# The last four units of an output stage run by token halves, and the next stage's whole half 0 is normed and split behind half 1

## The reference, cut to what matters

```
for li in range(2):
    m = mixer(rms_norm(x, g[0]))            # layer 0: gMLP, layer 1: RG-LRU
    x = x + rms_norm(m, g[1])
    f = (silu(h @ w_g) * (h @ w_u)) @ w_out # h = rms_norm(x, g[2])
    x = x + rms_norm(f, g[3])
```

## Time and profile before

| | us |
|---|---|
| median of 3 runs | 1548.31 |
| lowest and highest | 1547.86, 1551.93 |
| the profiled execution, its own time | 1548.71 |
| its span | 1547.2 |
| PE busy in the span | 1504.1 (97%) |
| DVE, ACT, POOL busy | 1072.6, 698.4, 328.0 |
| granted TensorE clock, mean over the span | 0.989 of full speed |

### The profile page before, as it was taken

One profiled execution on the slowest core, in us unless ns is written; L12 is line 12 of the kernel. 1 busy time (PEld: TensorE's weight loads), 2 busy tenths in 40 slices (PEclk: granted clock), 3 DMA queues, 4 the chain that ended last, 5 costly groups with the idle time before them and its releaser, 6 DMA issues.

```text
span 1547.2 us, 28460 instructions
## 1 busy us (share of the span) xinstructions
PE 1504.1 (97%) x10818; PEld 1477.8 (96%) x10818; DVE 1072.6 (69%) x1481; ACT 698.4 (45%) x1099; POOL 328.0 (21%) x282
## 2 busy tenths in 40 slices
PE   7999999999999999999999998999999999999997
PEld 7999999999999898999999998999989999999996
DVE  6454576766344689999963538967579999975434
ACT  5344432224343455555552534484555555554433
POOL 0100033333000332222210004724133222220003
PEclk9999999999999999999999999999999999999998
DMA  7322233232222112232242341312203423233211
GB/s 236 103 78 67 80 108 92 83 97 86 74 91 83 55 55 83 82 108 81 81 136 70 96 110 37 100 42 88 77 14 82 109 81 108 81 96 108 87 39 65
DMA packets 170507, 133.48 MB, mean 86 GB/s; under 512 B 4888, under 2 KB 147504, under 8 KB 170292
## 3 DMA queue, kind: packets, MB, share of 16 engines
q1 hardware_dynamic: 168756, 128.30, 27.8%
q0 software_dynamic: 1664, 3.95, 0.9%
HBM read 128.92 MB, written 3.29 MB: 85 GB/s over the span
## 4 chain that ended last, share of the span: by engine, by line
PE 87%; DVE 8%; issue 2%; ACT 1%; DMA 1%; POOL 0%; SPq 0%; DVEq 0%; ACTq 0%
PE ps L545 62%; PE ps L834 25%; DVE acc L1345 1%; DVE hl L1376 1%; DVE yb L1589 1%; DVE slo L1724 1%; DVE wide L1589 1%; DMA stage<-in_ffn_w_in_dram 1%; DVE acc L1355 1%; DVE wlo L1659 0%; DVE mixc L1642 0%; DMA wide<-in_x_prompt_dram 0%; PE ps L615 0%; DVE mixc L1641 0%; ACT whi L957 0%
## 5 line engine op out<-in xcount | busy, mean ns | idle before, releaser
L545 PE MATMUL ps<-hh,whi 128*128 128x288 f32 x2112 | 552.1, 300 | 13.7 <-DVE hl L1376 6.7
L545 PE MATMUL ps<-hh,wlo 128*128 128x288 f32 x2112 | 543.9, 296 | 0.0
L545 PE MATMUL ps<-hl,whi 128*128 128x288 f32 x2112 | 543.2, 296 | 0.0
L545 PEld LDWEIGHTS ps<-hh,whi 128*128 128x128 f32 x2112 | 372.1, 189 | 21.5 <-DVE hl L1376 10.3
L545 PEld LDWEIGHTS ps<-hl,whi 128*128 128x128 f32 x2112 | 372.2, 190 | 0.6
L545 PEld LDWEIGHTS ps<-hh,wlo 128*128 128x128 f32 x2112 | 372.5, 190 | 0.0
L1328 DVE TENSOR_TENSOR wlo<-stage,whi 128x1024 fp32r<-128x1024 f32 (+2 forms) x168 | 195.3, 1169 | 252.3 <-ACT whi L957 252.0
L957 ACT ACTIVATE whi<-stage 128x1024 fp32r<-128x1024 f32 (+2 forms) x168 | 165.3, 994 | 401.4 <-PE ps L545 382.4
L834 PE MATMUL ps<-shi,whi 128*128 128x288 f32 x576 | 170.5, 296 | 5.8 <-ACT tmp L1195 5.8
L834 PE MATMUL ps<-slo,whi 128*128 128x288 f32 x576 | 170.9, 297 | 0.0
L834 PE MATMUL ps<-shi,wlo 128*128 128x288 f32 x576 | 170.7, 296 | 0.0
(11 more groups left out here) (196 smaller groups left out, 2281.7 us busy)
## 6 DMA issues: line engine op xcount, KB each, us to landing
stage<-in_ffn_w_in_dram SPq DMA_DIRECT2D x88, 512.0 KB, 4.1
stage<-in_ffn_w_out_dram SPq DMA_DIRECT2D x40, 512.0 KB, 4.5
stage<-in_gm_w_in_dram SPq DMA_DIRECT2D x32, 384.0 KB, 3.9
stage<-in_gm_w_in_dram SPq DMA_DIRECT2D x24, 512.0 KB, 3.7
stage<-in_gm_w_out_dram SPq DMA_DIRECT2D x24, 512.0 KB, 3.7
stage<-in_rg_w_in_dram SPq DMA_DIRECT2D x16, 512.0 KB, 4.5
stage<-in_rg_w_out_dram SPq DMA_DIRECT2D x8, 512.0 KB, 3.9
wide<-in_x_prompt_dram SPq DMA_DIRECT2D x2, 1024.0 KB, 7.4
```

The lines of the kernel that those rows point to most:

```text
L545: return pe.matmul(out, w, x, start=start, stop=stop)
```

## The change

In the second group (G = 1) of every output stage the last four units run by token halves, not the last two (in RO, which has four units, the last three). So half 0 is complete four half-units before half 1 (three in RO). The splits of the next stage's tiles 0, 1 and 2 move behind the end of the units whose slots they take: the first, second and third of the four, in half 1. All eight `normed` and all eight `low` of half 0 move ahead of the four `post_add` of half 1 on DVE, and the `high` of half 0 likewise moves on ACT between and ahead of half 1's `y_out`. A new semaphore counts half 0's copies out, and PE's first tiles wait for it, and for half 1's copies only when they come to half 1. No computation is added or removed. In DMA, the loads of tiles 4 to 6, which wait for the low split of tiles 0 to 2, are issued later.

The diff, cut to its core:

```
-                    for j in range(per - 2):
+                    split = max(per - 2 - 2 * G, 1)
+                    for j in range(split):
...
-                        for j in (per - 2, per - 1):
+                        for j in range(split, per):
...
-                                if (G, h, j) == (1, 1, per - 2):
-                                    if m == 1:
-                                        post_sums(p, 0)
-                                    if m == 3:
-                                        post_spread(p, 0)
+                                if (G, h, j, m) == (1, 1, split, 1):
+                                    post_sums(p, 0)
+                                if (G, h, j, m) == (1, 1, split, 3):
+                                    post_spread(p, 0)
...
-                    pe.wait_ge(pair_free[m], free0[name][m])
+                    pe.wait_ge(y_half_out, 8 * p + 4 + m + 1)
...
+                        if k == 0:
+                            pe.wait_ge(pair_free[m], free0[name][m])
                         part(m, 1, k)
...
                                     post_std(p, 0)
                                     if NEXT[name]:
-                                        split_hi(n + 3)
+                                        split_hi(n + 1)
                                     post_rb(p, 0)
                                     if NEXT[name]:
                                         high(NEXT[name], 0, 0)
-                                if (G, h, m) == (1, 1, 1) and NEXT[name]:
-                                    high(NEXT[name], 0, 1)
+                                        split_hi(n + 2)
+                                        high(NEXT[name], 0, 1)
+                                        high(NEXT[name], 0, 2)
+                                        split_hi(n + 3)
+                                        for k in range(3, 6):
+                                            high(NEXT[name], 0, k)
+                                if (G, h) == (1, 1) and m < 2 and NEXT[name]:
+                                    high(NEXT[name], 0, 6 + m)
...
                                     post_diag(p, 0)
+                                    if NEXT[name]:
+                                        split_lo(n + 1)
                                     normed(p, 0, 0, add=x0_ready if NEXT[name] else x_last[0])
                                     if NEXT[name]:
                                         normed(p, 0, 1)
-                                        split_lo(n + 3)
                                         low(NEXT[name], 0, 0)
-                if NEXT[name]:
-                    normed(p, 0, 2)
+                                        split_lo(n + 2)
+                                        for k in range(1, KD):
+                                            if k + 1 < KD:
+                                                normed(p, 0, k + 1)
+                                            low(NEXT[name], 0, k)
+                                            if k == 2:
+                                                split_lo(n + 3)
...
                 for k in range(1, 4):
-                    normed(p, 0, k + 2)
-                    low(name, 0, k)
                     post_add(p, 1, 1, k)
-                normed(p, 0, 6)
-                low(name, 0, 4)
+                split_lo(n + 3)
                 post_diag(p, 1)
-                normed(p, 0, 7)
-                low(name, 0, 5)
-                split_lo(n + 3)
-                low(name, 0, 6)
                 normed(p, 1, 0)
                 normed(p, 1, 1)
-                low(name, 0, 7)
```

More of the change, by code:

```diff
@@ L296, in trunk_kernel @@
         ptok_done, pstd_ready, prtok_ready = sem("post_tok_done"), sem("post_std_ready"), sem("post_rtok_ready")
+        y_half_out = sem("first_half_copied_out")
         pdiag_ready, pbc_done, prb_ready = sem("post_diag_ready"), sem("post_bc_done"), sem("post_rb_ready")
@@ L796, in first_tiles @@
                         pe.wait_ge(lo_ready, n + 4)
-                        pe.wait_ge(pair_free[3], free0[name][3])
+                        pe.wait_ge(y_half_out, 8 * p + 8)
                         for before in range(k):
@@ L1004, in y_out @@
                 y_copy = act.activation(yo(p, r)[:, half(h)], src, ACT.Copy)
-                if h == 1:
-                    y_copy.then_inc(pair_free[m], 1)
+                y_copy.then_inc(pair_free[m] if h else y_half_out, 1)
             def h_high(k, layer, i, at):
@@ L1114, in out_phase @@
                     n = base[name] + s
-                    if n > base["GO"] and n + 2 < base["END"]:
+                    if n > base["GO"] and n + 2 < base["END"] and s + 2 < 2 * per:
                         split_hi(n + 2, width_of(n + 2))
@@ L1152, in first_tiles @@
                 j, p, n = PRE[name], PRE[name] - 1, base[name]
-                high(name, 0, 2)
                 act.wait_ge(unit_done, n)
                 y_out(p, 1, 1, 3)
-                high(name, 0, 3)
                 post_std(p, 1)
-                high(name, 0, 4)
                 split_hi(n + 3)
-                high(name, 0, 5)
                 post_rb(p, 1)
-                high(name, 0, 6)
-                high(name, 0, 7)
                 for k in range(KD):
@@ L1559, in out_phase @@
                     n = base[name] + s
-                    if n + 2 < base["END"]:
+                    if n + 2 < base["END"] and s + 2 < 2 * per:
                         split_lo(n + 2, width_of(n + 2))
```

## The result

The changed kernel takes 1553.38 us in the median of 20 runs, the kernel before 1548.88 in 20 runs beside them: a ratio of 1.0026, with a 95% interval of 1.0019 to 1.0033. That is 4 us slower: a small loss, but its interval lies wholly above 1. The forecast was 1552.3, its range 1545 to 1557.

A forecast was written before the change was run, and what follows sets the result against it. PE was taken as the bound, movable only in its idle time and slow stretches; the three transitions gave -0.1, +2.4 and +2.4 us, their last piece -0.7, together +4.0 on 1548.7; as median 1552.3, range 1545 to 1557.

The forecast's parts named there:

- P: Start of PE's token sums of half 1 in each transition; forecast 1.8, 1.8 and 3.0 us later than before.
- piece 4: From half 1's last `low` to the next `rb`; half of one half-clock loss of 1.5 us goes away, -0.7 us.
- Half 0's lead: First transition: half 0's last square comes 6.24 us earlier, of which 4.4 are left at the first `normed`.
- PE's wait and the clock: Before half 1's sums, PE's scattered waits become one of about 5.5 us, and the clock falls each time.
- P to S: From the start of half 1's token sums to half 1's first `normed`; forecast 6.4 us in each transition.
- its floor of 5.0: Least time from half 1's sums to its first `normed`: sums, split, root, diagonal, spread and `rb`, 5.0 us.
- The rival in which the clock stays: Clock holds behind PE's wait, sums to half 1's first `normed` take 5.0 us: 1548.1 us, chance 0.13.
- Piece 3: From half 1's first `normed` to its last `low`; one `low` of half 0 is gone from it, -0.4 us.
- What was counted as free: Last unit's weights, later DMAs of tiles 4 to 6 and POOL's earlier adds cost nothing; FO1 gains nothing.
- The rival in which the lead is kept: DVE runs its pairs without waiting for ACT and POOL, and the clock stays: 1540.7 us, chance 0.14.

The follow-up runs named there:

- depth2: The changed kernel with PE's order of before: two units by halves in place of four (three in RO); ACT and DVE orders unchanged; 1563.35 us, 1.0087.
- adds_first: The changed kernel with half 1's squares on ACT and adds on DVE ahead of half 0's `high` and `low` 3 to 7; 1543.94 us, 0.9958.
- filler: The changed kernel with 40 more matmuls on PE just ahead of half 1's token sums, in its 5.6 us wait; 1548.52 us, 0.9994.
- sums_later: The changed kernel with PE's token sums of half 1 behind k = 4 instead of 2, the spread behind k = 5 instead of 4; 1550.10 us, 1.0003.
- split_behind: The changed kernel with tile 0's low split on DVE behind the first `normed` and its residual add, in the first two transitions; 1552.78 us, 1.0022.
- before_adds: The kernel before with half 1's squares ahead of `high` 1 to 3, its adds ahead of `low` 1, PE's sums and spread one step earlier; 1550.03 us, 1.0010.
- adds_first_d2: adds_first with PE's order of before: two units by halves in place of four (three in RO); 1564.11 us, 1.0094.
- before_adds_hold: before_adds with the extra matmuls of hold in the last steps of half 1; 1551.15 us, 1.0007.
- hold: adds_first with extra matmuls on PE where it waits for `low` in the last steps of half 1; 1538.13 us, 0.9928.
- hold_sb: hold and split_behind together, with the edits of both; 1538.94 us, 0.9924.

## Why the prediction was right

The direction, the mechanism and the size were right; two terms of the sum were mis-sized. P came 1.6 us later over the three transitions than forecast and piece 4 was 2.3 us shorter; that they nearly cancel is luck.

- **Half 0's lead.** Forecast: last square 507.23, tile 0's split 511.03, first `normed` 513.3, first `low` 514.8. Measured 507.44, 511.24, 513.48 and 515.09, with an entry 0.14 later. From the entry 4.4 of 6.24 us were left, as forecast. depth2 shows that the lead is real, adds_first where it goes.
- **P, mis-sized.** +1.8, +1.8 and +3.0 were forecast, +2.2, +2.2 and +3.7 measured, inside the bounds of +3.0 and 4.2. The last `low` ended 0.2 later in its place, behind four waits of DVE of 0.28 to 0.29 us for ACT's `high`, and the last square waited 0.42 for the first add. 0.1 is a slip in the sum: 528.2 and 2.0 make 530.2, not 530.1. The third transition lost 0.25 more because its first `normed` came 2.9 us earlier than before (14.89 from the entry for 17.79), 1.46 less than in the first transition, where 1.2 had been counted. 0.2 of that is tile 0's split, which needs no unit of half 1 there but still stands between the diagonal and the `normed` on DVE: from half 0's sums to the `normed` it is 3.0 us, for 2.8 before.
- **PE's wait and the clock.** One wait of about 5.5 forecast, 5.6 measured, and the clock fell in all three. P to S was taken at 6.4 and measured at 6.3, 6.1 and 7.1, and its floor of 5.0 was met by filler to 0.04 us. The rival in which the clock stays did not happen; filler shows what it would have given: 0.9994 of the kernel before, or 1 us less, where 1548.1 had been worked out, 0.2 less. The three transitions after differ in when the clock rose again: from 3.3 to 5.3 us behind P it was at 0.61 and 0.72, and at 0.50 in the third.
- **Piece 3.** -0.4 forecast, -0.41 to -0.46 measured.
- **Piece 4, mis-sized.** -0.7 forecast, with -3.0 as the bound; the bound was met. In piece 3 PE is busy for 15.30 of 15.62 us, where it had waited 1.5 of 16.20. PE's waits at the end of half 1, before and after:

```profile
551.31 0.40 PE L545 MATMUL ps<-hh,whi 128*128 128x288 f32 x1 [1.04 <-DVE hl L1376]
...
552.41 0.40 PE L545 MATMUL ps<-hh,whi 128*128 128x288 f32 x1 [0.44 <-DVE hl L1376]
...
552.74 0.40 PE L546 MATMUL ps<-hh,whi 128*128 128x288 f32 x1 [0.44 <-DVE hl L1378]
```

The wait of 1.04 is gone, in all three transitions. The other kernels go the same way: with the 0.44 alone the clock of piece 4 held in 17 of 18 transitions (changed kernel, filler, sums_later, depth2, split_behind and before_adds), with the 1.04 ahead of it in 2 of 9 (before, adds_first and adds_first_d2). That is a strong sign, not a rule. I had counted half of one of the two falls away.

- **What was counted as free** was free: PE waited 2.08 us in FO1 before its sums for 2.18 before, and did not wait for the last units' weights. Tile 2's late split did make PE wait 1.5 us in RO to FI1, inside time that the longer wait would have taken anyway.
- **The rival in which the lead is kept** needed P by 529 with the order as it was. It did not come, and split_behind shows that moving one split does not bring it. It takes another order: adds_first.

The Trainium skill ("TensorE: Matmul & The Clock Gate", "HAM oscillation") says that PE restarts at half rate after a long wait. The rows agree for the three waits of 5.6 us after and for those of 3.48 in before_adds (0.50 to 0.56 behind them); behind the 3.28 in sums_later PE restarted at full clock and fell a little later. The 2.89 us in FI0, which the prediction held against it, are shorter than each of these and settle nothing, and in adds_first the clock fell behind waits of no more than 1.04.

## What to carry to other kernels

Bringing one half forward is worth only what the other half's chain does not lose: on an engine that runs its list in order, put the few short steps that another engine's queue hangs on (here four adds, 2.1 us in all) ahead of the bulk for which nobody waits yet. Ahead of a step for which PE did wait, in before_adds, they gained nothing. In the kernels run here the lead with its first order and the order on the kernel before each gave nothing, together they gave 6 us, and 11 with PE kept at work; not every order was tried with either. Where a wait can't be avoided, price the clock behind it, see where an engine that is now earlier will wait next, and fill only waits that are there: extra matmuls in their place cost time (before_adds_hold).

## What the hardware showed that I had not expected

In adds_first PE has the same five waits at the end of half 1 in all three transitions (2.2 to 2.3 us in all, none longer than 1.04). The clock stayed at 1.00 behind them in the first and fell to 0.63 in the two others. In before_adds it fell in the third transition behind a single wait of 0.43; behind the same wait it stayed at 1.00 in the first two. So waits of one size and order don't decide it alone; what else does, no run here tells. Filling them with matmuls whose results nobody reads held it each time (hold and hold_sb).
